# Expert stages of a two-block model on one core: gate and up products with the weights stationary, and their halves added by VectorE

## The reference, cut to what matters

```
# x: the tokens of expert e; gate, up: 1024 x 512; down: 512 x 1024
g = silu(x @ exp_w_gate[e]) * (x @ exp_w_up[e])
y = g @ exp_w_down[e]          # weighted by the router and added to the token
```

## Time and profile before

| | |
|---|---|
| time, median of 3 runs | 2324.67 us (2324.57 to 2326.35) |
| the profiled execution | 2324.68 us, span 2322.9 us |
| granted TensorE clock, mean | 0.982 |
| PE busy | 2237.4 us (96% of the span) |
| PEld busy | 2029.4 us (87%) |
| DVE busy | 1546.2 us (67%) |
| ACT busy | 1099.2 us (47%) |
| gate and up products of the experts, moving low weights | 1008, mean 280 ns |
| low parts of expert units made by DVE | 192, mean 2290 and 2286 ns |

### The profile page before, as it was taken

How to read it: one execution, slowest core, us unless ns; L and a number is a source line. 1 busy time by engine, 2 the same in 40 slices (tenths; PEclk the granted TensorE clock), 3 DMA queues, 4 the chain that set the end, 5 groups by cost and what they waited for, 6 DMA issues and landing times.

```text
span 2322.9 us, 35509 instructions
## 1 busy us (share of the span) xinstructions
PE 2237.4 (96%) x15048; PEld 2029.4 (87%) x15048; DVE 1546.2 (67%) x1719; ACT 1099.2 (47%) x1408; POOL 6.7 (0%) x16
## 2 busy tenths in 40 slices
PE   9999999989999999989999979999999999999998
PEld 7888888768999999979999948899997978899997
DVE  4896596245777777527775343888886443888887
ACT  4221232243334433525344443677776454677775
POOL 0000000000000000000000000000000000000000
PEclk9999999999999999999999989999999989999999
DMA  8576777415886788437885512788886422688885
GB/s 308 193 245 245 259 256 268 162 46 180 302 298 245 265 298 308 164 119 262 305 301 183 182 37 91 270 295 301 297 323 236 146 72 91 228 299 307 311 308 216
DMA packets 126739, 535.50 MB, mean 231 GB/s; under 512 B 11744, under 2 KB 47912, under 8 KB 82416
## 3 DMA queue, kind: packets, MB, share of 16 engines
q1 hardware_dynamic: 124896, 524.33, 63.1%
q0 software_dynamic: 944, 5.72, 0.6%
q10 hardware_dynamic: 736, 3.10, 0.3%
HBM read 532.04 MB, written 1.06 MB: 230 GB/s over the span
## 4 chain that ended last, share of the span: by engine, by line
PE 87%; DVE 6%; ACT 4%; DMA 1%; issue 1%; SPq 0%; DVEq 0%; ACTq 0%
PE PS L893 16%; PE PS L1334 13%; PE PS L819 11%; PE PS L967 9%; PE PS L1368 7%; PE PS L915 7%; PE PS L1014 5%; PE PS L854 5%; DVE moe_low L2416 3%; PE PS L1292 2%; PE PS L788 2%; PE PS L1270 1%; PE PS L720 1%; PE PS L955 1%; DMA ring<-mod_w 1%
## 5 line engine op out<-in xcount | busy, mean ns | idle before, releaser
L893 PE MATMUL PS<-h_parts,FFN_HIGH 128*128 128x256 f32 x2112 | 383.1, 284 | 5.0 <-DVE h_parts L2018 5.0
L2416 DVE TENSOR_TENSOR moe_low<-moe_ring,W_HIGH 128x2048 fp32r<-128x2048 f32 x128 | 292.9, 2290 | 76.9 <-ACT W_HIGH L1785 76.9
L893 PEld LDWEIGHTS PS<-h_parts,FFN_HIGH 128*128 128x128 f32 x2112 | 329.0, 192 | 5.8 <-issue 5.5
L893 PE MATMUL PS<-h_parts,ring_low 128*128 128x256 f32 x1056 | 298.8, 283 | 0.0
L1334 PE MATMUL PS<-moe_low,HXH 128*96 128x256 f32 x1008 | 282.7, 280 | 0.0
L1785 ACT ACTIVATE W_HIGH<-moe_ring 128x2048 fp32r<-128x2048 f32 x128 | 244.6, 1913 | 23.0 <-PE PS L1368 22.7
L2045 DVE TENSOR_TENSOR ring_low<-ring,FFN_HIGH 128x2048 fp32r<-128x2048 f32 x99 | 226.6, 2291 | 40.2 <-ACT FFN_HIGH L1565 40.2
L2076 DVE SCALAR_TENSOR_TENSOR roots<-CB,cond_rows,roots 128x1024 f32<-128x1024 f32 x186 | 238.3, 1281 | 9.6 <-DVE roots L2076 0.9
L1565 ACT ACTIVATE FFN_HIGH<-ring 128x2048 fp32r<-128x2048 f32 x99 | 188.8, 1909 | 95.0 <-DMA ring<-down_w 89.1
L893 PEld LDWEIGHTS PS<-h_parts,ring_low 128*128 128x128 f32 x1056 | 202.6, 192 | 0.0
L1334 PEld LDWEIGHTS PS<-moe_low,HXH 128*96 128x96 f32 x1008 | 164.2, 163 | 0.3
(11 more groups left out here) (338 smaller groups left out, 4863.6 us busy)
## 6 DMA issues: line engine op xcount, KB each, us to landing
moe_ring<-moe_w SPq DMA_DIRECT2D x192, 1024.0 KB, 5.0
CB<-mod_rows SPq DMA_DIRECT2D x192, 512.0 KB, 6.0
ring<-up_w SPq DMA_DIRECT2D x88, 1024.0 KB, 5.0
ring<-lin_w SPq DMA_DIRECT2D x55, 1024.0 KB, 5.0
ring<-down_w SPq DMA_DIRECT2D x43, 1024.0 KB, 5.8
CB<-mod_dual SPq DMA_DIRECT2D x96, 128.0 KB, 2.6
ring<-mod_w SPq DMA_DIRECT2D x8, 1024.0 KB, 8.7
CB<-mod_rows SPq DMA_DIRECT2D x32, 128.0 KB, 2.7
```

What stands on the lines that cost most here:

```text
L893: return mm(PS[:, i % 2, h * S:(h + 1) * S], a[:, k, h * P:(h + 1) * P], b[:, k, :], start=start, stop=(k == KT - 1 and j == 2), skip_grou ...
L2416: tt(by_tile(moe_low[:, moe_slot(l, p), :]), by_tile(moe_ring[:, moe_slot(l, p), :]), w_high_tiles(p), ALU.subtract).then_inc(w_low, 1)
```

## The change

The gate and up units turn their operands round. A 128 x 128 tile of weights is stationary, and the slots are moved. The high and low parts of the slots stand in one tensor (`HX`) now, so one product with the high weights moves both, 192 columns; a second product, with the low weights, moves the 96 high slots. There are two halves (gate, up) of 8 tiles: 32 products in a unit. The result has the features as partitions, 96 columns of "high slots" and 96 of "low slots" for gate and for up. VectorE adds the two with one `tensor_reduce` into `SUMS` in SBUF, for gate and up together; ScalarE takes silu there; VectorE multiplies into `GT` in SBUF, which already lies as the down products want it, so `turn_products` is gone. The bank is free once the sum is made: PE waits on `mo_sums` where it waited on `mo_g`. `down_last`, behind the last unit, waits on it too. VectorE's order becomes sums, low part, gated for each unit.

```diff
-        GATE, GT = sg_flat[:, 0:DE], sg_flat[:, DE:2 * DE]
+
+        SUMS = pool_w[:, :, :].rearrange("p a b -> p (a b)")[:, 0:4 * CAP].rearrange("p (u c n) -> p u c n", u=2, c=2)
+        GT = sg_flat[:, 0:2 * ET * CAP].rearrange("p (e n) -> p e n", e=2)
+
+        def halves(f):
+
+            both = PS[:, 2 + f % 2, :].rearrange("p (c n) -> p c n", c=2)[:, :, 0:2 * CAP]
+            return both.rearrange("p c (a n) -> p c n a", a=2)
...
                     if 4 * (e0 + e) + f >= 2:
-                        pe.wait_ge(mo_g, 4 * (e0 + e) + f - 1)
+                        pe.wait_ge(mo_sums, 4 * (e0 + e) + f - 1)
...
-                        pairs = ((XH, high), (XH, low), (XL, high)) if p else ((XH, high), (XL, high))
-                        for i, (a, w) in enumerate(pairs):
-                            last = mm(PS[0:CAP, 2 + f % 2, 0:S], a[:, x], w[:, k, :],
-                                      start=(k + i == 0), stop=(k + i == KT + 1), skip_group_check=True)
...
+                        dst = PS[:, 2 + f % 2, c * S:c * S + 2 * CAP].rearrange("p (a n) -> p a n", a=2)
+                        return mm(dst, high[:, k, c * P:(c + 1) * P], HX[group % 2][:, :, slots(k)], start=(k + c == 0),
+                                  stop=False, skip_group_check=True)
+
+                    def by_low(c, k):
+                        return mm(PS[:, 2 + f % 2, c * S:c * S + CAP], low[:, k, c * P:(c + 1) * P], XH[:, slots(k)],
+                                  start=False, stop=(k == KT - 1), skip_group_check=True)
+                    if p:
+                        for c in range(2):
+                            for k in range(KT):
+                                by_high(c, k)
+                                last = by_low(c, k)
...
                     gate_up(e, 0)
-                    if e:
-                        turn_products(e - 1)
                     gate_up(e, 1)
                     if e:
                         down_products(e - 1)
-                        pe.wait_ge(mo_g, 4 * (e0 + e) + 2)
+                        pe.wait_ge(mo_sums, 4 * (e0 + e) + 2)
                         turn_list(e)
...
                 def gate(e, f):
-                    act.wait_ge(unit_done, u0 + MOE_AT[e, f] + 1)
-
-                    if 4 * (e0 + e) + f >= 4:
-                        act.wait_ge(mo_g, 4 * (e0 + e) + f - 3)
-                    af(GATE[0:CAP, f * P:(f + 1) * P], PS[0:CAP, 2 + f % 2, 0:P], ACT.Silu)\
-                        .then_inc(mo_silu, 1)
+                    act.wait_ge(mo_sums, 4 * (e0 + e) + f + 1)
+                    af(SUMS[:, f % 2, 0, :], SUMS[:, f % 2, 0, :], ACT.Silu).then_inc(mo_silu, 1)
 
                 def turned(e):
-                    act.wait_ge(mo_gtpsum, e0 + e + 1)
-                    af(GXH[:, :], PS[:, 0, 0:ET * CAP], ACT.Copy).then_inc(mo_gthigh, 1)
+                    act.wait_ge(mo_g, 4 * (e0 + e) + 4)
+                    af(GXH[:, :], GT[:, e % 2, :], ACT.Copy).then_inc(mo_gthigh, 1)
...
+                def sums(e, f):
+                    dve.wait_ge(unit_done, u0 + MOE_AT[e, f] + 1)
+                    dve.tensor_reduce(SUMS[:, f % 2, :, :], halves(f), AX.X, ALU.add).then_inc(mo_sums, 1)
+
                 def gated(e, f):
                     dve.wait_ge(mo_silu, 4 * (e0 + e) + f + 1)
...
-                    tt(GT[0:CAP, w], GATE[0:CAP, w], PS[0:CAP, 2 + f % 2, P:2 * P], ALU.mult)\
+                    tt(GT[:, e % 2, f * CAP:(f + 1) * CAP], SUMS[:, f % 2, 0, :], SUMS[:, f % 2, 1, :], ALU.mult)\
                         .then_inc(mo_g, 1)
...
-                    gated(e, 0)
+                    sums(e, 0)
                     if e:
                         turned(e - 1)
                     split(MOE_AT[e, 0] + 3)
+                    gated(e, 0)
                     if e + 1 < NE:
                         place(e + 1)
+                    sums(e, 1)
+                    split(MOE_AT[e, 1] + 3)
                     gated(e, 1)
-                    split(MOE_AT[e, 1] + 3)
...
+                    sums(e, 2)
+                    split(MOE_AT[e, 2] + 3)
                     gated(e, 2)
-                    split(MOE_AT[e, 2] + 3)
-                    gated(e, 3)
+                    sums(e, 3)
                     if part < 3:
                         split(MOE_AT[e, 3] + 3)
+                    gated(e, 3)
```

More of the change, by code:

```diff
@@ L400, in program @@
                              "mo_silu", "mo_g"))
-        place_ready = sem("place_ready")
-        mo_gtpsum, mo_gthigh, mo_gtready, mo_yhigh, mo_y = (
-            sem(n) for n in ("mo_gtpsum", "mo_gthigh", "mo_gtready", "mo_yhigh", "mo_y"))
+        place_ready, mo_sums = sem("place_ready"), sem("mo_sums")
+        mo_gthigh, mo_gtready, mo_yhigh, mo_y = (
+            sem(n) for n in ("mo_gthigh", "mo_gtready", "mo_yhigh", "mo_y"))
         y_psum, y_half = sem("y_psum"), sem("y_half")
@@ L537, in program @@
         HTL = (rounded("HTL0", CB_at + KT * WIDE * 4, [P, D]), rounded("HTL1", late_at + KT * WIDE * 4, [P, D]))
-        HXH = (rounded("HXH0", CB_at, [P, KT * WIDE]), rounded("HXH1", G_at, [P, KT * WIDE]))
-        HXL = (rounded("HXL0", late_at, [P, KT * WIDE]), rounded("HXL1", G_at + KT * WIDE * 4, [P, KT * WIDE]))
+        pair_step = (late_at - CB_at) // 4
+        HX = (rounded("HX0", CB_at, [P, 2, pair_step]), rounded("HX1", G_at, [P, 2, KT * WIDE]))
+        HXH, HXL = ([x[:, i, 0:KT * WIDE] for x in HX] for i in range(2))
         at = 2 * KT * WIDE
@@ L1315, in gate_up @@
                     group, part = e // GROUP, e % GROUP
-                    XH, XL = HXH[group % 2], HXL[group % 2]
+                    XH = HXH[group % 2]
                     p = MOE_AT[e, f]
@@ L1324, in gate_up, with slots @@
                     if 4 * (e0 + e) + f >= 2:
-                        pe.wait_ge(mo_g, 4 * (e0 + e) + f - 1)
+                        pe.wait_ge(mo_sums, 4 * (e0 + e) + f - 1)
                     if f == (3 if e else 1):
                         pe.wait_ge(mo_tready, e0 + e + 1)
-                    for k in range(KT):
-                        if part == 0 and f == 0 and k >= KT - 2:
+                    def slots(k):
+                        return slice(k * WIDE + part * CAP, k * WIDE + (part + 1) * CAP)
@@ L1330, in gate_up, with by_high @@
+                    def by_high(c, k):
+                        if part == 0 and f == 0 and c == 0 and k >= KT - 2:
                             pe.wait_ge(mo_gathered, 32 * l + KT * group + k + 1)
-                        x = slice(k * WIDE + part * CAP, k * WIDE + (part + 1) * CAP)
-                        pairs = ((XH, high), (XH, low), (XL, high)) if p else ((XH, high), (XL, high))
-                        for i, (a, w) in enumerate(pairs):
-                            last = mm(PS[0:CAP, 2 + f % 2, 0:S], a[:, x], w[:, k, :],
-                                      start=(k + i == 0), stop=(k + i == KT + 1), skip_group_check=True)
@@ L1336, in gate_up @@
-                    if p == 0:
+                        dst = PS[:, 2 + f % 2, c * S:c * S + 2 * CAP].rearrange("p (a n) -> p a n", a=2)
[4 more added lines that the diff above has]
+                                  start=False, stop=(k == KT - 1), skip_group_check=True)
@@ L1337, in gate_up @@
+                    if p:
[3 more added lines that the diff above has]
+                                last = by_low(c, k)
+                    else:
+                        for c in range(2):
+                            for k in range(KT):
+                                by_high(c, k)
                         pe.wait_ge(w_low, v0 + 1)
[L1338 to L1341, removed]
+                        for c in range(2):
+                            for k in range(KT):
+                                last = by_low(c, k)
@@ L1342, in gate_up @@
                     last.then_inc(unit_done, 1)
[L1344 to L1353, removed]
@@ L1375, in down_last @@
                     e = NE - 1
+                    pe.wait_ge(mo_sums, 4 * (e0 + e) + 4)
                     for _ in range(7):
@@ L1415, in moe @@
                 spilled = pe.value_load(over[0:1, 0:1], min_val=0, max_val=1)
-                turn_products(NE - 1)
                 down_last()
@@ L2436, in outputs @@
                             in1=YGH[0:CAP, w], op0=ALU.mult, op1=ALU.subtract).then_inc(mo_y, 1)
+                def sums(e, f):
+                    dve.wait_ge(unit_done, u0 + MOE_AT[e, f] + 1)
+                    dve.tensor_reduce(SUMS[:, f % 2, :, :], halves(f), AX.X, ALU.add).then_inc(mo_sums, 1)
                 def gated(e, f):
                     dve.wait_ge(mo_silu, 4 * (e0 + e) + f + 1)
-                    w = slice(f * P, (f + 1) * P)
-                    if f == 0 and e0 + e:
-                        dve.wait_ge(mo_gtpsum, e0 + e)
-                    tt(GT[0:CAP, w], GATE[0:CAP, w], PS[0:CAP, 2 + f % 2, P:2 * P], ALU.mult)\
+                    tt(GT[:, e % 2, f * CAP:(f + 1) * CAP], SUMS[:, f % 2, 0, :], SUMS[:, f % 2, 1, :], ALU.mult)\
```

(3 more changed lines are left out.)

## The result

The changed kernel takes 2630.11 us (median of 4 runs, 2622.45 to 2635.82); the kernel before took 2324.62 us beside it. The ratio is 1.1318 (95% interval 1.1299 to 1.1338): 13% slower, some 305 us. That is inside the forecast range of 2500 to 2635 us, but 63 us above the forecast of 2567, above the likeliest case's own range (2540 to 2610), and 5 us above what the clock rival gave (2625). One execution of a later kernel, the one with the low weights' products widened, ran at a mean granted clock of 0.586 and took 3887.53 us; it is left out of every comparison.

The account below looks back on a forecast made before the run. PE was taken to bound the kernel, VectorE close behind. Per layer +10.5 (first expert), +80 (eleven middle) and +30 (last four) make +121, twice +242 on 2324.68: 2567 us, range 2500 to 2635.

Parts of the forecast that it names:

- the likeliest case: Whole kernel: VectorE and ScalarE take turns, PE keeps full clock; 28.2 us per expert, 2567 us in all, chance 0.75.
- the clock rival: PE in expert stages: waits drop the clock, at 1.2 GHz 55% of the time; +58 us, 2625 us; chance 0.12.
- the turns: Gate and up units: VectorE idles through each ScalarE high part, since gate waits for the sum; 8.5 us per expert.
- PE's unit: Gate and up unit on PE: 32 products paced by loads, 3.8 us (bounds 3.6 and 3.8), 1.0 more than before.
- Idle ahead of a low part: VectorE per unit, waiting for ScalarE's high part: 2.16 us; at an expert's first unit 0.77 before GXL, 1.25 after.
- some 6: Sign in the waits: VectorE's low part waits for ScalarE's high part some 6 us more per expert than before.
- if the granted clock leaves 1.00 there: Sign in the expert stages that the forecast is wrong: PE's granted clock falls below 1.00, as in the clock rival.
- against: ... the new products move six to twelve times 16 columns: Argument against the clock rival (chance 0.12): PE's new products move more columns than the 16-column ones seen at clock 0.82.
- half clock makes an expert's PE time 34.5 us: Price within the clock rival: at 1.2 GHz a unit takes 4.5 us, so PE passes 28.2 above 38% of the time.
- Loads alone: PE's loads decide, high parts run ahead of gates: 24.4 us per expert, +112, 2437 us; chance 0.08.
- The other side: Busy time alone decides, loads hide behind narrower products: VectorE's 19.7 us per expert sets the pace, 2287 us; chance 0.03.

Follow-up runs that it names:

- both orders mended: Changed kernel with ScalarE's high part ahead of the gate and the low weights' products moving 192 columns instead of 96: 2399.67 us, 1.0328.
- fills of 512 columns: Changed kernel with spare PE products, 4 ahead of the down products and 9 ahead of the third unit of each expert: 2563.23 us, 1.1030.
- the first experiment: Changed kernel with only ScalarE's order changed, the next weights' high part ahead of the gate in each unit: 2421.71 us, 1.0432.
- the turns alone: Kernel before, its own products kept, with a VectorE copy of the bank ahead of each ScalarE gate in the changed kernel's order: 2547.62 us, 1.0975.

## Why the prediction was right, and where it was short

**The account.** From the medians: the loads, 2400 - 2323 = 77 us (both orders mended, clock kept); the turns, 2545 - 2400 = 145 (the low products wide in both); the clock, 2630 - 2545 = 85. They make 307 for the 305 measured. The order of steps matters here: turns and clock are not independent, since without the turns PE hardly idles.

**PE's unit: right, at the lower bound.** 16 pairs of 0.223 us are 3.57 us for the 3.8 taken, with 3.6 as the bound. The starts were expected to be evenly spaced behind 192 and 96 columns; they are 0.16 and 0.07 us in turn, and only their mean, 0.1116, is as expected. An expert in which PE never idles takes 23.33 us; the forecast had 24.4 (its own terms add up to 24.5, and to 23.6 at the lower bound), and four units of 0.23 us less make 23.5. The Trainium skill (TensorE: Matmul & The Clock Gate, section LDWEIGHTS) has a load take its columns over 1.2 GHz, which makes 107 ns for 128 columns and 80 for 96 (estimates from that page); the rows show 0.1116 and 0.090, in the same direction and a little more each.

**The turns: right, and the likeliest.** The kernel with the widened low products has the turns and no lasting falls, so it can be held against the forecast window by window: the first expert, the next eleven, the last four of a layer.

```profile
1453.90:1482.68 28.78, 23.39 (x184) 22.90 (x184) 19.40 (x21) 9.83 (x13) 0.00 (x0) 0.94 0.57 200
1482.68:1786.50 303.82, 274.09 (x1949) 248.37 (x1950) 211.54 (x224) 162.67 (x199) 0.00 (x0) 0.96 0.63 225
1786.50:1887.92 101.42, 88.34 (x638) 79.39 (x637) 69.50 (x70) 53.93 (x62) 0.00 (x0) 0.97 0.65 236
```

28.78 us for a forecast 31.1; 303.82/11 = 27.6 per expert for 28.2; 101.42 for 104.6. Twice the differences are 23 us, the 22 by which the forecast lay too high. Idle ahead of a low part is 2.15 us (2.16 forecast), and 0.76 and 1.25 around GXL (0.77 and 1.25). The sum takes 0.55 us as taken, 0.48 of it on the chain. The difference lies mostly in VectorE's busy time, 211.54/11 = 19.2 us per expert where 19.7 was expected, and 19.40 in the first where it was 21.7; the idle time, 8.4 us, is what was expected (8.5). The waits agree: VectorE's low part waits for ScalarE 242.5 us in 130 waits, 76.9 in 98 before, which is 5.2 us more per expert ("some 6"). In the changed kernel itself the first expert took 32.52 us, at a clock of 0.63.

**The clock: taken for a rival with a chance of 0.12, and there.** The prediction named "if the granted clock leaves 1.00 there" as a sign of being wrong, and it did. The forecast rests on the likeliest case without the clock, and that case was measured: 2545 and 2563 us with the clock mostly held up, for 2567. The changed kernel's 2630.11 is outside that case's own range; it lies within the stated one only because the clock rival had taken the upper end to 2635. What failed is the term that the sum put at nothing, some 85 us for the clock, and with it the rival's weighing, in two places. The first is "against: ... the new products move six to twelve times 16 columns". The width of products does matter, far above 16 columns: the same kernel with 192 columns throughout has no lasting falls, and fills of 512 columns avoid most. The second is its price, "half clock makes an expert's PE time 34.5 us", by a unit of 4.5 us in which the 96-column product keeps the load's 0.12. In the fall two high products start 0.43 us apart:

```profile
1553.24 0.49 PE L1344 MATMUL PS<-HX,h_parts 128*128 128x192 f32 x1
1553.53 0.34 PE L1348 MATMUL PS<-HX,moe_low 128*128 128x96 f32 x1
1553.67 0.49 PE L1344 MATMUL PS<-HX,h_parts 128*128 128x192 f32 x1
```

Over a unit it is 0.427, 1.9 times the 0.223 at full clock. That is 16 x 0.427 = 6.8 us a unit and not 4.5: the time of a pair behind two loads of 128 columns nearly doubles with the clock, so the load cannot have kept its 0.11 us. The Trainium skill (TensorE: Matmul & The Clock Gate, section LDWEIGHTS) gives one figure for the load and names no clock; here the measurement decides. So a far smaller part of the time at 1.2 GHz makes PE the bound again. An estimate: all of PE's 23.33 us at 1.9 times would be some 44 us, and PE passes 27.5 at (27.5 - 23.3)/(44 - 23.3) = 20% and not at 38%. The fourth expert fits: PE's 23.33 us at a granted 0.79 are 29.5 us, where PE was busy for 29.11, and the 3.2 in which it still idled make the 32.29. At 0.79 a slow expert spends 42% of its time at 1.2 GHz; over the 15 whole experts of a layer the clock of 0.85 and 0.87 means 30 and 26%, and not the 55% priced. The rival's 2625 came close by luck: its price at half clock was too low, its share of the time too high, and its base 22 us too high.

**The other rivals fell.** Loads alone (2437) need VectorE to idle under 4.7 us per expert; it idles 8.5 (27.47 - 18.99). What that rival describes is the first experiment, where the high part may run ahead: 2421.71. The other side (2287) fell with the load: the narrower products don't start closer together.

**Left open.** Kernels that differ in one of the two say this much: with gaps and wide products (the turns alone, the low products widened) the clock falls and is soon back; with narrow products and no gap it doesn't fall, but once it has fallen behind a gap it stays down under them. Why the clock comes back when it does, and what narrower or wider products than these would do, was not tried.

## What to carry to other kernels

When an edit puts a new producer between two in-order queues, follow the loop that closes through both: a short operation (0.55 us here) can cost several times itself, because what stands behind the waiting instruction can't start; then look for what can be issued ahead of the wait. Count stationary loads before moved columns: halving the columns of a product (192 to 96) saved nothing here, where its load was the longer of the two. And price PE's idle time by the clock too: the same turns cost 85 us more with products of 96 columns in every pair than with 192 throughout, so once PE waits, look at the granted clock and at the shape of the products behind the gap.

## What the runs showed of the hardware

- The spacing of fp32r products behind loads of 128 columns was 0.1116 us in the mean at full clock, with 192 and 96 columns moved in turn as with 192 throughout, and 0.213 at the 1.2 GHz level (192 and 96 in turn). Behind loads of 96 columns, with 192 moved, it was 0.090.
- With PE busy without a gap, products of 192 and 96 columns in turn kept a clock of 1.00 (first experiment, 1489.98 to 1513.31 us), but did not bring it back from 0.50 between 1462 and 1482 us; with 192 columns throughout it was back by 1462.
- In the changed kernel the clock that had fallen behind a gap at 1548 us stayed at 0.50 from 1554 until 1566 with PE busy throughout, under narrow products and scatter's 16 of 256 columns, and was rising (0.83 in the next 2 us) while the gathers' products of 384 columns ran. Adding columns, or whole products without use, made the kernel faster, by 85 and 67 us.
